# Turning over the identity on TensorE in nine of its waits, in a two-block transformer kernel on one core

## What is computed

```python
def reference(...):
    x = first_block(x, ...)
    return second_block(x, ...)

def first_block(...):
    # layer 0: gated delta rule (8 heads, chunks of 64), then a SwiGLU of width 2816
    # layer 1: windowed attention (16 heads), then 8 experts of width 3584, the best 2 per row
    for i in range(DEPTH):
        h = gated_deltanet(x, ...) if i % 2 == 0 else swa_sink_attention(x, ...)
        x = layer_norm(ALPHA * x + h, ...)
        f = swiglu(x, ...) if i % 2 == 0 else moe_swiglu(x, ...)
        x = layer_norm(ALPHA * x + f, ...)
    return x

def second_block(...):
    for l in range(DEPTH):
        h = rmsnorm(x, norm_g[l])
        proj = h @ w_in[l]              # q, k, v, gates, an index of 16 heads, rnn inputs
        attn = dsa_attention(q, k, v, iq, ik, iw)
        y_a = (attn * silu(ga)) @ w_out_attn[l]
        hr = rg_lru(causal_depthwise_conv_2(xr, ...), ...)
        y_b = (hr * silu(gr)) @ w_out_rnn[l]
        merged = sigmoid(ma) * y_a + sigmoid(mb) * y_b
        x = x + merged @ w_o[l]
    return rmsnorm(x, final_g)
```

## Time and profile before

| | before |
|---|---|
| median of three executions | 2320.51 us |
| the profiled execution | 2316.55 us |
| its span, from the first to the last instruction | 2314.4 us |
| TensorE products busy | 2206.8 us (95%) |
| TensorE weight loads busy | 1954.5 us (84%) |
| VectorE busy | 1760.8 us (76%) |
| ScalarE busy | 1468.9 us (63%) |
| mean granted clock of TensorE | 0.985 |

### The profile page before, as it was taken

How to read it: one execution, slowest core, us unless ns; L and a number is a source line. 1 busy time by engine, 2 the same in 40 slices (tenths; PEclk the granted TensorE clock), 3 DMA queues, 4 the chain that set the end, 5 groups by cost and what they waited for, 6 DMA issues and landing times.

```text
span 2314.4 us, 35167 instructions
## 1 busy us (share of the span) xinstructions
PE 2206.8 (95%) x14207; PEld 1954.5 (84%) x14207; DVE 1760.8 (76%) x2214; ACT 1468.9 (63%) x1954; POOL 326.6 (14%) x314
## 2 busy tenths in 40 slices
PE   7789999988999999999999999969999999999998
PEld 7778999867888888888888888859898998989898
DVE  5634655788999999989898999964589666379865
ACT  5432444556877777777777878753575845466754
POOL 0510000000000000000000000003556200555500
PEclk9999999998999999999999999989999999999999
DMA  9522655517999999999999999946545365655452
GB/s 252 134 74 74 234 186 173 182 65 253 334 341 387 362 358 353 356 355 365 351 364 348 367 342 367 373 168 200 177 146 164 113 221 155 215 163 149 139 154 102
DMA packets 328401, 556.48 MB, mean 240 GB/s; under 512 B 23616, under 2 KB 164680, under 8 KB 328232
## 3 DMA queue, kind: packets, MB, share of 16 engines
q1 hardware_dynamic: 318432, 527.63, 65.6%
q0 software_dynamic: 9120, 25.97, 4.7%
q10 hardware_dynamic: 680, 0.54, 0.1%
HBM read 544.12 MB, written 9.96 MB: 239 GB/s over the span
## 4 chain that ended last, share of the span: by engine, by line
PE 77%; DVE 14%; ACT 6%; issue 3%; DMA 0%; SPq 0%; ACTq 0%; DVEq 0%
PE bank L856 23%; PE bank L858 22%; PE bank L857 22%; DVE parts L2435 4%; ACT parts L1806 2%; PE bank L862 1%; PE bank L1522 1%; DVE work L3189 1%; PE bank L1008 1%; DVE fast L2435 1%; PE bank L1583 1%; DVE work L3206 1%; DMA raw<-in_a_w_in_dram 0%; ACT work L2363 0%; PE bank L1730 0%
## 5 line engine op out<-in xcount | busy, mean ns | idle before, releaser
L2435 DVE TENSOR_TENSOR parts<-raw,parts 128x1024 fp32r<-128x1024 f32 (+1 forms) x713 | 858.3, 1219 | 385.9 <-ACT parts L1806 363.0
L1806 ACT CAST parts<-raw 128x1024 fp32r<-128x1024 f32 (+1 forms) x713 | 732.8, 1035 | 502.7 <-PE bank L858 486.7
L856 PE MATMUL bank<-cols,parts 128*128 128x256 f32 x1680 | 494.4, 294 | 8.9 <-DVE parts L2435 5.4
L858 PE MATMUL bank<-cols,parts 128*128 128x256 f32 x1680 | 479.1, 285 | 2.9 <-issue 2.9
L857 PE MATMUL bank<-cols,parts 128*128 128x256 f32 x1680 | 479.5, 285 | 0.0
L2435 DVE TENSOR_TENSOR fast<-raw,fast 128x1024 fp32r<-128x1024 f32 x302 | 362.0, 1219 | 32.0 <-ACT fast L1806 14.8
L1806 ACT CAST fast<-raw 128x1024 fp32r<-128x1024 f32 x302 | 315.8, 1052 | 95.0 <-PE bank L858 87.3
L856 PEld LDWEIGHTS bank<-cols,parts 128*128 128x128 f32 x1680 | 326.5, 194 | 22.5 <-issue 18.6
L857 PEld LDWEIGHTS bank<-cols,parts 128*128 128x128 f32 x1680 | 326.7, 194 | 4.9 <-issue 4.1
L858 PEld LDWEIGHTS bank<-cols,parts 128*128 128x128 f32 x1680 | 326.5, 194 | 0.0
L856 PE MATMUL bank<-parts,cols 128*128 128x512 f32 x740 | 295.1, 399 | 13.6 <-DVE parts L2435 6.9
(11 more groups left out here) (384 smaller groups left out, 3498.8 us busy)
## 6 DMA issues: line engine op xcount, KB each, us to landing
raw<-in_moe_w_gate_dram SPq DMA_DIRECT2D x112, 1024.0 KB, 7.4
raw<-in_moe_w_up_dram SPq DMA_DIRECT2D x112, 1024.0 KB, 7.1
raw<-in_moe_w_down_dram SPq DMA_DIRECT2D x112, 1024.0 KB, 7.2
raw<-in_w_in_dram SPq DMA_DIRECT2D x76, 1024.0 KB, 5.5
raw<-in_a_w_in_dram SPq DMA_DIRECT2D x12, 1024.0 KB, 12.3
raw<-in_ffn_w_gate_dram SPq DMA_DIRECT2D x11, 1024.0 KB, 5.2
raw<-in_ffn_w_up_dram SPq DMA_DIRECT2D x11, 1024.0 KB, 5.2
raw<-in_ffn_w_down_dram SPq DMA_DIRECT2D x11, 1024.0 KB, 4.9
```

The costliest lines, as they stand in the source:

```text
L856: pe.matmul(o, l[0], r[0], start=start, stop=False)
L858: return pe.matmul(o, l[1], r[0], start=False, stop=stop)
L1806: a.copy(dst[0], src).then_inc(*up(o + "hi", x))
L2435: v.tensor_tensor(dst[1], src, dst[0].bitcast(F32), ALU.subtract).then_inc(*up(o + "lo", x))
```

## The change

A new helper claims a bank and multiplies the identity by four copies of itself into the whole bank, n times. No event is raised. It is called in nine places of TensorE's program, named a to i here; the call in `index_steps` (i) runs once in each of the two layers of the second block, and the one after `own` (d) once for each of two groups of heads.

```diff
+        def spin(n, b):
+
+            claim(b)
+            for _ in range(n):
+                pe.matmul(v3(bank[b][:, :], 4), ident, ident.unsqueeze(1).broadcast_to([128, 4, 128]), start=True, stop=True)
+
         def tr(o, i):
...
         tr(bank[5][:, 128:202], pr2[0:74, :]).then_inc(*up("par"))
         busy[5] = ("par_rows",)
+        spin(6, 3)
...
             def inv_b(lv):
                 for gi in range(4):
                     b = 6 + gi % 2
+                    if lv == 1 and gi == 0:
+                        spin(4, b)
                     pe.wait_ge(*at("inv_m", lv, gi))
...
             yield
             yield
+            spin(8, 5)
             sums(5, 0)
...
                 for hg in range(2):
                     own(c + 1, hg)
+                    if c == 0:
+                        spin(1, 7)
         turn_o(0)
...
         busy[5] = ("logits",)
+        spin(5, 7)
         pe.wait_ge(*at("sel"))
...
         busy[7] = ("ranked",)
+        spin(3, 5)
...
             if l == 0:
+                spin(27, 0)
                 h_cols(0, 0)
+                spin(4, 1)
...
                 yield
+                spin(3, 4)
                 pe.wait_ge(*at("roped", l, "iq", 6))
```

## The result

The changed kernel took 2331.15 us (median of six, 2327.73 to 2336.72) beside 2320.63 us for the kernel before on the same chip: a ratio of 1.0049, 95% interval 1.0037 to 1.0061. So it is slower, by 10.5 us, and inside the forecast range. The forecast said 2339 and +18.6 us: the direction and the largest term were right, the total nearly twice the measured one. The two profiled executions differ by more, 2316.55 to 2331.74 us, +15.2.

What follows compares the result with a forecast made beforehand. The prediction took TensorE, carrying 77% of the chain of waits, to bound the kernel. Its place-by-place delays and clock gains summed to +18.6 us, added to the median of 2320.51: 2339.1 us, range 2327 to 2348.

Steps and rivals of the forecast that it cites:

- The price of a turn: One turn on TensorE costs 0.86 us at full clock and 1.71 at half, from the equal shape at L1670.
- Rival 1: A turn costs only 0.43 us, so turns fit almost everywhere: -7.4 us, 2313 us; chance 5%.
- Place g: 27 turns before h_cols(0,0): 15.8 us late, less 1.9 us for h_cols at full clock.
- Rival 2: The overrun before h_cols(0,0) is partly covered by weights split ahead: 2328 us; chance 8%.
- Place b: 4 turns in inv_b, level 1: +3.4 us in front of products VectorE waits for; the 2.66 us wait stays.
- Place d: Two turns after own(1, hg), with no idle time there: +2.6 us.
- Places c, e, f and a: c, before sums(5,0): -0.5 us; e, before "sel", and f, by the L1522 gathers: together 0; a, after the first transposes: 0.
- Place h: 4 turns in the 2.53 us wait before 1560.07: cost +0.9 us, clock gains -1.6 and -0.8.
- The base: The sum was added to the median, 2320.51 us, giving 2339.1; on the profiled run, 2316.55 us, it gives 2335.2.
- i: 3 turns in each layer, in waits of 1.8 us: cost +1.5 us, clock gain -0.8, together +0.7.
- rival 3: The turns do nothing to the clock: no gains of 12 us, about +31 us, 2351 us; chance 6%.
- Its cap of 1.1%: All eleven low-clock stretches vanishing could return at most 26 of 2314.4 us; this caps the gain, not the loss.

Runs made afterwards that it cites:

- half: The changed kernel with every turn cut to 256 columns, all counts and places kept: 2317.96 us, ratio 0.9993 to the kernel before.
- g0: The changed kernel without the 27 turns before h_cols(0,0), all other turns kept: 2316.89 us, ratio 0.9985 to the kernel before.
- No_b: The changed kernel without the 4 turns in inv_b, level 1: 2328.72 us, ratio 1.0032 to the kernel before.
- No_d: The changed kernel without the two turns after own: 2331.91 us, ratio 1.0039 to the kernel before.
- only_g: The kernel before with only the 27 turns before h_cols(0,0) added: 2329.94 us, ratio 1.0039 to the kernel before.
- fit: The changed kernel with turn counts cut to fit the idle time, 9 before h_cols(0,0), none after own: 2312.36 us, ratio 0.9967 to the kernel before.
- g9: The changed kernel with 9 turns instead of 27 before h_cols(0,0): 2319.60 us, ratio 0.9993 to the kernel before.

## Why the prediction was right, and where it was too high

**The price of a turn** was right: 0.86 us at full clock, 1.7 to 2.0 at half, from the one row of equal shape. Rival 1, the turn at 0.43 us, falls by the kernel after (records 0.43 us apart, two to a turn) and was made real by half. Its 2313 us was too low even there, measured 2318; in part by its own sum, for its terms add up to -6.3 and not -7.4, which is 2314. Nor do 216 ns for 512 columns hold here, the figure of the Trainium skill (TensorE: Matmul & The Clock Gate, Back-to-back issue gap): for this plain float32 operand the trace has four times as much a turn.

**Place g** was right as a term: late 15.8 us forecast, 15.8 in the profile, less 1.7 for h_cols. The step that carried it was to count the usable part of the 13.4 us wait from the branch on the earlier trace rows: the turns began at 1544.99, after 3.83 us of idle time. Rival 2, cover at g by work done ahead, falls by g0: taking the 27 turns away gave back 14 to 15 us.

**Place b** was the step of the working that failed: +3.4, with the wait and the half clock behind it kept. In the profile the wait was gone. I had read that L1008 waited for VectorE's update, and had not asked what VectorE did ahead of it: a split of 2.81 us, which VectorE can do while TensorE turns. No_b shows the wait at 1.25 us beside the turns at a and c. By these profiles the turns cost about +2, and the stretch gained 2.9 us without them, for a reason that stays open.

**Place d.** The stretch added +5.5 where +2.6 was forecast, but this is not the turns' price. They ran wholly at half clock, 2.0 us each. No_d and only_g have no turns there and add 3.2 us, by 13.65 us of low clock instead of 6.82. The turns themselves come to 2.2 us, close to the term; what the sum lacked is the longer low stretch.

**Places c, e, f and a** came out as reckoned or better. At a the turns ended 0.2 us late, counted from the start of the span, instead of 2.5: the clock rose at 12.8 us, 2.6 us after the first turn, where I took 3.9 to 5.6; at e it rose 3.2 us after.

**Place h** gained 2.3 us for 1.5, but only_g has the same gain with no turns at h, so the cost of +0.9 and its gains were put at the wrong place: the turns at g bring the gain. The 0.5 us at the start and the 1.3 us near 57 us that the kernel after gained stood in no term; that was luck.

**The base** was the second failed step, and about as large. I added a sum worked out on one execution of 2316.55 us to the median of 2320.51. Against its own base the sum came nearer: 2335.2 forecast, 2331.74 in the execution profiled, in part because terms that were too high (b by 4.2 us, a by 1.4, i by 1.3, h by 0.8) met costs that had no term (3.2 us of low clock at d, 3.1 at 1631 and 1955). The execution of before had 20.5 us of low stretches between 30 and 200 us; only_g, whose code is the same up to 1540 us, had 27.3 and was 2.8 us later at 200 us. The kernel after's profile is at its own median, so 4 of the 8 us by which I was high are this. By medians the failed part is the eight other places: without g the forecast had them at +4.7 us, g0 measured them at -3.5 (-6.3 to -0.7), and the ratios of after and only_g at about +2, with wider intervals.

**The gains of clock.** The prediction speaks of 12 us; its own gains, place by place, add up to 13.9, so rival 3 stood at +32.5 and not +31. Its cap of 1.1% is also a little above the 1% that it is set beside, not under it. Low stretches that went after c, g and in e and f gave about what their terms said. But others fell elsewhere, at 480, 1631, 1771 and 1955 us; those at 1631 and 1955 cost about 1.5 us each. The profile of fit shows the same on its side: ten low stretches with 40.6 us of work in them, where before has 52.4, so 5.9 us of clock gained and not 12 or more. It gains 7 us in the median.

What stays open: what b and d cost in the median, what made the split at b short in some kernels, and why 1.1 to 3.1 us of idle time with no named release end at 55 to 60 us in all profiles of this study but that of no_d.

## What to carry to other kernels

Work that fills a wait is free only up to what the wait holds after the branch, and TensorE pays the rest in full: price one unit by a row of the same type and width, and divide the usable time by it. Before counting low clock as a loss, look at the busy time inside the low stretches: 15.8 of the 68.3 us here were idle, all of it in two stretches of eleven. Before crediting a gain to the work put in beside it, look for the same gain in a kernel without that work, as at h and d. And a sum worked out on one execution belongs on that execution, above all when the gain sought is no larger than the spread between executions.

## What the runs showed of the hardware that I had not expected

The clock also fell with no idle time before it. In the kernel after it fell at 1630.7 us, 4.6 us after TensorE began 32 narrow products of 16 and 32 columns without a gap, followed by wide ones; before, it fell at 533.70, 3.2 us into such a series of 8 and 16 columns (its one gap was 0.02 us). No turn stands near the fall at 1630.7. That the narrow width is the reason isn't tested.

```profile
1626.14 0.18 PE L958 MATMUL bank<-parts,cols 128*128 128x32 f32 x1
1626.17 0.26 PE L959 MATMUL bank<-parts,cols 128*128 128x16 f32 x1
...
1629.63 0.36 PE L856 MATMUL bank<-cols,parts 128*128 128x256 f32 x1
```

Reading the flag and branching over the overflow stage stand in 3.3 to 3.8 us of idle time on TensorE, with nothing named that ends it, in all eight kernels with turns at g (3.83 in the kernel after, 3.78 in fit, 3.41 in g9, 3.26 in half). A second idle time of 0.5 to 1.4 us stands three records later in three of the eight. In the kernel after, the only transfers between 1540 and 1545 us are three packets of the instruction queues, so the loading of code may be part of it; no run shows that.
